# A two-block transformer on one core: the pooling sums and the mean subtraction of the mixers move from GpSimd to VectorE

## The chip, the cores and the metric

The kernel runs on one core of a Trainium2 chip, in one launch. The metric is the device time of the whole program in microseconds (us). Engines are written as the profile writes them: PE (TensorE matmul), PEld (TensorE weight load), DVE (VectorE), ACT (ScalarE), POOL (GpSimd), SP (SyncE, which here only issues DMAs).

## The reference, cut to what matters

A first transformer block (two layers) and a second one (two layers) are worked one after the other in float32 on 256 tokens of 1024 channels. Only the first block is touched. Each of its layers is a feed-forward network, a mixer, and a second feed-forward network, each followed by a layer norm of a weighted sum of input and output; 16 learned tokens are put ahead of the 256, so that the rows are 272 long. The mixer has three branches over one projection of its input:

```python
z = h @ w_in
xp, ca, cg, q, k, v, g = jnp.split(z, splits, axis=-1)
y_pool = pool_mixer(xp, pool_w, pool_scale)      # trailing means over 2, 4, 8, 16 tokens, minus the token
y_conv = conv_module(ca, cg, ...)                # 31-tap causal depthwise convolution, norm, projection
y_ret = retention(q, k, v, g, ret_gn_g)          # four heads with a decay, then a norm per head
return jnp.concatenate([y_pool, y_conv, y_ret], axis=-1) @ w_out
```

The pooling branch takes, for each of four groups of 64 channels, the mean over the last 2, 4, 8 or 16 tokens, subtracts the token itself and multiplies the result with a small matrix.

## The kernel before, in words

Every engine has its own instruction stream, written out by hand and run in order; the streams are tied by semaphores (`then_inc` when an instruction is done, `wait_ge` ahead of one that needs it). There is no planner: the place of a line in an engine's stream is its order.

Activations lie channel-major: 128 partitions by 8 tiles of channels (`CT`) by 272 tokens (`L1`). Weights stream as "units" of 1 MB (128 x 2048 float32). For each unit SP issues a DMA into one of four slots of `RAW`, ACT rounds it to `WHI` (function `high`, L1430), and DVE subtracts to get the low part `WLO` (function `rest`, L1975). Each product is three matmuls: high by high, high by low, low by high (function `three`). A slot is loaded again when PE has finished the unit in it.

A mixer has 15 units, `u0` to `u0 + 14`. PE's stream in it (function `mixer` under `block.tensor`) is: units 0 and 1 (the convolution's input and gate), units 2 to 5 (queries and keys), units 6 and 7 (values, token-major) with `scores(0)` and `scores(1)` of the retention heads behind them, unit 8 (the pooling branch's input), `values(0)`, `scores(2)`, `values(1)`, unit 9 (half of the output gate), the pooling product "pooled" (`PW` by `PM`), `scores(3)`, `values(2)`, the mean of the convolution's output (`ONES` by `ACC`, semaphore `cv_mean`), the first tile of unit 10, the variance (`ONES` by `CSG`, semaphore `cv_var`), `values(3)`, the second tile of unit 10, the variance of the heads (`ONES` by `OSQ`), the convolution's projection, and units 11 to 14, the output projection, with the sums for the norm after them.

`scores(h)` writes a head's scores into PSUM banks 4 to 6, so that `scores(h)` waits until DVE has taken the scores of head h - 1 out of them (DVE function `decay(h - 1)`, L2192 and L2193, semaphore `ret_decayed`). The mean of the convolution waits for all 62 taps (semaphore `conv_tap`) and for the low parts of the pooling output (`YPL`, L2252, semaphore `y_low`).

DVE's stream in a mixer (function `mixer` under `block.vector`) interleaves four things: `rest` of each unit, the 62 taps of the convolution (`taps(a, b)`, L2171, two instructions of 128 x 272 for each tap), the rotation of queries and keys (`rotate(n)`, L2182 to L2186), and `decay(h)`. In the part that matters its order is `taps(7, 14)`, `decay(0)`, `centre_values(0)`, `taps(14, 21)`, `rest(u0 + 10)`, `centre_values(1)`, `decay(1)`, `rest(u0 + 11)`, `taps(21, 28)`, `decay(2)`, `taps(28, 31)`, `rest(u0 + 12)`, the two `YPL`, `decay(3)`, and then the norms of the convolution and of the heads (`CSTD`, L2262; `GSTD`, L2269; `GS`, L2278; `XLO`, L2272 and L2281).

POOL works in a mixer: the loads of tables, `add_halves` (L521, L524: sum over the channels' tiles in `SUM1`, for a mean that PE takes and ACT copies to `MH`), `shift_x` (L532: four instructions, `PL = XL - MH`, after all four rotations, since the rotation's scratch tiles lie in `PL`), the pooling windows (L586 to L593), and, after the output projection, `add_tiles` (L543). The windows need `XP`, which ACT copies out of PSUM when unit 8 is done (L1562). They are four running sums, each of the one before it (windows of 2, 4, 8, 16 tokens, `PT_`), four products with the inverse counts on 64 partitions each (`WN`), and one subtraction (`PM`): nine instructions, counted by the semaphore `pool_step`, on which PE's pooling product waits. `PL` is needed by `take_tiles` (L2055), which adds the output projection to it, and waits on `x_shifted`.

A `Steps` object counts instructions on one semaphore; `link` issues an instruction and waits for it, `did` only counts it:

```python
def link(self, ins):
    self.did(ins)
    self.wait()
```

Of the kernel before, what the change touches and what calls it, by code (L numbers as in the profile page):

```python
# [11 lines left out]
ALU = mybir.AluOpType  # L12
# [12 lines left out]
L1 = META + SEQ  # L25
# [22 lines left out]
POOL_STEPS = 9  # L48
# [23 lines left out]
def build(nc, A, out):  # L72
    with ExitStack() as ctx:
        def sem(name):
            return ctx.enter_context(nc.semaphore(name))
# [42 lines left out]
        XL = X[:, :, X0:L2]  # L118
# [7 lines left out]
        MH = norm.put("MH", [L1])  # L126
# [32 lines left out]
        IC = mixb.put("IC", [2, L1])  # L159
        PW = mixb.put("PW", [2, P])  # L160
        PWC = mixb.put("PWC", [4, P])
        XP = mixb.put("XP", [2, 16 + L1])
        YPH = place("B", "YPH", mixb.at, [2, L1], F32R)
        YPL = place("B", "YPL", mixb.at + 2 * L1, [2, L1], F32R)
        PT_ = [mixb.put(f"PT{n}", [2, 16 + L1]) for n in range(4)]
        WN = mixb.put("WN", [2, L1])
        PM = mixb.put("PM", [2, L1])
# [128 lines left out]
        def tokens(q):  # L296


            return slice(META if q >= 4 else 0, L1)
# [7 lines left out]
        def conv_at(i, f):  # L307
# [12 lines left out]
        half_added, half_mean, half_copied, x_shifted = (sem("half_added"), sem("half_mean"), sem("half_copied"),  # L320
                                                         sem("x_shifted"))
# [5 lines left out]
        tab1_loaded, pads_set = sem("tab1_loaded"), sem("pads_set")  # L327
        conv_gate, conv_in, conv_tap, rot_step, rotated = (sem("conv_gate"), sem("conv_in"), sem("conv_tap"),
                                                           sem("rot_step"), sem("rotated"))
# [3 lines left out]
        xp_copied, pool_step, pooled = sem("xp_copied"), sem("pool_step"), sem("pooled")  # L333
# [41 lines left out]
        for n in range(UNITS1):  # L375
            l, m = n // UNITS_LAYER, n % UNITS_LAYER
# [73 lines left out]
        def bc(t, n):  # L450
            return t.rearrange("p (o n) -> p o n", o=1).to_broadcast([P, n, t.shape[-1]])
# [42 lines left out]
        def _(pool):  # L494
# [3 lines left out]
            def ada_load(h):  # L498
                if h >= ADA_RING:
                    pool.wait_ge(ada_step, 8 * (h - ADA_RING + 1))  # L500
                pool.dma_start(AW[:, h % ADA_RING, :, :], A["ada"][h, :, :].rearrange("p (k c) -> p k c", k=4))\
                    .then_inc(ada_loaded[h % ADA_RING], 16)
# [24 lines left out]
            def shift_x(q):  # L527

                pool.wait_ge(half_copied, q + 1)
                tk = tokens(q)  # L530
                for c in range(4):
                    pool.tensor_tensor(PL[:, 2 * c:2 * c + 2, tk], XL[:, 2 * c:2 * c + 2, tk], bc(MH[:, tk], 2),  # L532
                                       ALU.subtract).then_inc(x_shifted, 1)
# [29 lines left out]
            def mixer(l):  # L563
                q, base = 3 * l + 1, POOL_STEPS * l
                pool.wait_ge(ada_done, 6 * (2 * l + 1))
                for dst, src in ((RC[:, :], A["rope_c"]), (RS[:, :, :], A["rope_s"]), (DT[:, :, :, :], A["decay"]),
                                 (IC[:, :, :], A["inv_count"]), (PW[:, :, :], A["pool_w"][l, :, :, :]),
                                 (PWC[:, :, :], A["conv_pw"][l, :, :, :])):
                    pool.dma_start(dst, src).then_inc(tab1_loaded, 16)
                pool.wait_ge(tile_out, 8 * q)  # L570
                pool.memset(CP[:, :, 0:TAPS - 1], 0.0).then_inc(pads_set, 1)
                pool.memset(XP[:, :, 0:16], 0.0).then_inc(pads_set, 1)
                for t in PT_:
                    pool.memset(t[:, :, 0:16], 0.0).then_inc(pads_set, 1)
                add_halves(q)
                pool.wait_ge(rotated, 4 * l + 4)
                shift_x(q)
                pool.wait_ge(xp_copied, l + 1)
                pool.wait_ge(pads_set, 6 * (l + 1))
                pool.wait_ge(tab1_loaded, 16 * 6 * (l + 1))  # L580
                st = Steps(pool, pool_step, base, POOL_STEPS)
                src, n = XP, 16 + L1
                for j in range(4):
                    w = 1 << j
                    lo = 2 * w - 1
                    st.link(pool.tensor_tensor(PT_[j][:, :, lo:n], src[:, :, lo:n], src[:, :, lo - w:n - w], ALU.add))  # L586
                    src = PT_[j]
                for j in range(4):
                    q64 = slice(64 * (j % 2), 64 * (j % 2) + 64)
                    st.did(pool.tensor_tensor(WN[q64, j // 2, :], PT_[j][q64, j // 2, 16:n], IC[q64, j // 2, :],  # L590
                                              ALU.mult))
                st.wait()
                st.did(pool.tensor_tensor(PM[:, :, :], WN[:, :, :], XP[:, :, 16:n], ALU.subtract))  # L593
                st.end()
                add_tiles(q)
                for h in range(ADA_RING):
                    if h == 2:
                        pool.wait_ge(tile_out, 8 * q + 8)
                    ada_load(12 * (2 * l + 1) + h)
# [35 lines left out]
            for odd in range(2):  # L635
                pool.wait_ge(pool2_step, QUERY_SET - 2 + odd)
                q = slice(64 * odd, 64 * odd + 64)
# [18 lines left out]
            for n in range(2):  # L656
                for odd in range(2):
                    pool.wait_ge(pool2_step, HEADS_ZERO + 2 * n + odd)
                    q = slice(64 - 64 * odd, P - 64 * odd)
# [1306 lines left out]
        def _(v):  # L1966
            v.memset(MODF[:, :, :], 0.0).then_inc(start_set, 1)

            def rest(n):

                if n >= UNITS:
                    return
                s = slot_of[n]
                v.wait_ge(w1_high, highs[n])
                v.tensor_tensor(WLO1[:, s, :], RAW[:, s, :], WHI1[:, s, :].bitcast(F32), ALU.subtract)\  # L1975
                    .then_inc(w1_split, 1)
# [39 lines left out]
            def pair(c, tk):  # L2016
                return PL[:, 2 * c:2 * c + 2, tk]
# [135 lines left out]
            def mixer(l):  # L2153
                q = 3 * l + 1
# [7 lines left out]
                def taps(a, b):  # L2162
                    for t in range(a, b):
                        for j in range(2):
                            w = VEC[:, V_DW + 2 * t + j:V_DW + 2 * t + j + 1]
                            if t == 0:
                                ins = v.tensor_scalar(ACC[:, j, :], CP[:, j, 0:L1], w,
                                                      VEC[:, V_DB + j:V_DB + j + 1], ALU.mult, ALU.add)
                            else:
                                v.wait_ge(conv_tap, l * 62 + (2 * t + j - 1))  # L2170
                                ins = v.scalar_tensor_tensor(ACC[:, j, :], CP[:, j, t:t + L1], w, ACC[:, j, :],  # L2171
                                                             ALU.mult, ALU.add)
                            ins.then_inc(conv_tap, 1)
# [22 lines left out]
                def centre_values(z):  # L2196
# [10 lines left out]
                        last = v.tensor_tensor(o, o, m, ALU.add)  # L2207
                    last.then_inc(v_centred, 1)

                def head_gain(h):  # L2210
                    v.wait_ge(ret_squared, 4 * l + h + 1)
                    v.wait_ge(gs_done, 2 * l + h // 2 + 1)
                    v.scalar_tensor_tensor(GS[:, h, :], OT[:, h, :], VEC[:, V_GN + h:V_GN + h + 1], GS[:, h, :],
                                           ALU.mult, ALU.mult).then_inc(gn_z, 1)
# [28 lines left out]
                centre_values(1)  # L2243
                decay(1)
                rest(u0 + 11)
                taps(21, 28)
                decay(2)
                taps(28, 31)
# [9 lines left out]
                head_gain(0)  # L2258
                head_gain(1)
                rest(u0 + 13)  # L2260
                v.wait_ge(cv_std, l + 1)
                v.reciprocal(CSTD[:, :], CSTD[:, :]).then_inc(cv_rstd, 1)  # L2262
                v.wait_ge(cv_rstd, l + 1)
                v.wait_ge(cv_squared, l + 1)
                v.tensor_tensor(ACC[:, :, :], ACC[:, :, :], bc(CSTD[:, :], 2), ALU.mult).then_inc(cv_normed, 1)
                head_gain(2)
                head_gain(3)
                v.wait_ge(gn_std, l + 1)
                v.reciprocal(GSTD[:, :], GSTD[:, :]).then_inc(gn_rstd, 1)  # L2269
                for t in range(2):  # L2270
                    v.wait_ge(y_high, 8 * l + 3 + t)
                    v.tensor_tensor(XLO1[:, 2 + t, :], PS[:, t, 0:L1], XHI1[:, 2 + t, :].bitcast(F32), ALU.subtract)\  # L2272
                        .then_inc(y_low, 1)
                for h in range(RH + 1):
                    if h < RH:
                        v.wait_ge(gn_spread, 4 * l + h + 1)
                        v.wait_ge(gn_z, 4 * l + h + 1)
                        v.tensor_tensor(GS[:, h, :], GS[:, h, :], PS[:, 4 + h, 0:L1], ALU.mult).then_inc(gn_y, 1)  # L2278
                    if h >= 1:
                        v.wait_ge(y_high, 8 * l + 4 + h)  # L2280
                        v.tensor_tensor(XLO1[:, 3 + h, :], GS[:, h - 1, :], XHI1[:, 3 + h, :].bitcast(F32),  # L2281
                                        ALU.subtract).then_inc(y_low, 1)
# [565 lines left out]
```

## Time and profile before

| what | value |
|---|---|
| median of 3 runs | 2326.58 us (2322.51 to 2329.9) |
| the profiled execution's own time | 2322.65 us |
| span of its profile | 2320.9 us |
| granted TensorE clock, mean over the span | 0.969 |
| PE busy | 2216.4 us, 96% of the span |
| PEld busy | 2030.0 us, 87% |
| DVE busy | 1611.2 us, 69% |
| ACT busy | 1046.7 us, 45% |
| POOL busy | 209.8 us, 9% |
| bytes moved | 333.86 MB, mean 144 GB/s |

The span is the time from the first to the last instruction that the profile holds; the execution's own time is 1.75 us longer. Busy shares are means over all stages, so the stretches of the two mixers are read by themselves: the first lies at about 240 to 385 us, the second at about 820 to 960 us of the span. A granted clock of 1.00 is TensorE's 2.4 GHz, one of 0.50 is 1.2 GHz; a number between them is a stretch that had both.

### The profile page before, as it was taken

The page shows a single profiled execution, that of the slowest core. Times are in us where ns is not written, and L with a number is a line of the kernel's source. Part 1 is how long each engine was busy: PE and PEld are TensorE (multiplying, and loading weights), DVE is VectorE, ACT ScalarE, POOL GpSimd, SP SyncE. Part 2 cuts the span into 40 slices and gives each one's busy share as a digit, 9 for nine tenths or more (in the row PEclk, how much of TensorE's full clock was granted, in tenths as well). Part 3 has the DMA queues.
Part 4 walks back from the last instruction along what each step waited for, and adds up shares of the span by engine and source line. Part 5 has one row for each costly group of instructions (what it writes and reads, how often), then busy time and mean ns, then how long its engine had stood idle before and what let it go on. Part 6 is the DMA issues. An engine that isn't in the chain of part 4 may idle for free. (4 is left out here: it accounts for less than half of the span.)

```text
span 2320.9 us, 35981 instructions
## 1 busy us (share of the span) xinstructions
PE 2216.4 (96%) x15136; PEld 2030.0 (87%) x15136; DVE 1611.2 (69%) x2407; ACT 1046.7 (45%) x1512; POOL 209.8 (9%) x219
## 2 busy tenths in 40 slices
PE   6999998999999999899999998999999997997997
PEld 6999978999999997899999776698888886687997
DVE  5878886877887789697853467666455437757774
ACT  5433535433544344444444335534444323755662
POOL 2100232100210023210100001000000000100000
PEclk9999989999999999999998999999999998998998
DMA  5665524667466552476522112022322222113552
GB/s 212 241 218 204 193 73 152 241 224 255 182 220 218 199 193 85 186 256 236 201 91 79 55 55 79 19 73 91 105 95 91 104 78 74 54 42 115 186 177 100
DMA packets 47488, 333.86 MB, mean 144 GB/s; under 512 B 5532, under 2 KB 6652, under 8 KB 7776
## 3 DMA queue, kind: packets, MB, share of 16 engines
q1 hardware_dynamic: 37808, 268.45, 32.3%
q0 software_dynamic: 9520, 63.11, 7.3%
q8 instruction: 120, 1.97, 0.3%
q14 instruction: 40, 0.33, 0.0%
HBM read 330.50 MB, written 1.05 MB: 143 GB/s over the span
## 5 line engine op out<-in xcount | busy, mean ns | idle before, releaser
L1975 DVE TENSOR_TENSOR WLO<-RAW,WHI 128x2048 fp32r<-128x2048 f32 x252 | 587.9, 2335 | 269.4 <-ACT WHI L1430 266.6
L448 PE MATMUL PS<-XB,WHI 128*128 128x256 f32 (+1 forms) x3072 | 701.0, 323 | 15.5 <-DVE XB L2320 10.7
L1430 ACT CAST WHI<-RAW 128x2048 fp32r<-128x2048 f32 x252 | 479.8, 1907 | 317.8 <-DMA RAW<-in_dn_c 79.8
L448 PEld LDWEIGHTS PS<-XB,WHI 128*128 128x128 f32 x3072 | 517.4, 192 | 62.8 <-issue 18.1
L448 PE MATMUL PS<-XHI,WHI 128*128 128x272 f32 (+1 forms) x1792 | 523.3, 295 | 18.3 <-ACT XHI L1438 14.9
L448 PE MATMUL PS<-XHI,WLO 128*128 128x272 f32 (+1 forms) x1792 | 518.1, 292 | 0.0
L448 PE MATMUL PS<-XLO,WHI 128*128 128x272 f32 (+1 forms) x1792 | 495.2, 290 | 0.0
L448 PE MATMUL PS<-XB,WLO 128*128 128x256 f32 (+1 forms) x1536 | 494.0, 322 | 0.0
L448 PEld LDWEIGHTS PS<-XHI,WHI 128*128 128x128 f32 x1792 | 346.3, 193 | 23.8 <-issue 18.8
L448 PEld LDWEIGHTS PS<-XHI,WLO 128*128 128x128 f32 x1792 | 345.8, 193 | 0.0
L448 PEld LDWEIGHTS PS<-XLO,WHI 128*128 128x128 f32 x1792 | 334.1, 192 | 0.4
L448 PEld LDWEIGHTS PS<-XB,WLO 128*128 128x128 f32 x1536 | 294.9, 192 | 21.1
L2006 DVE SCALAR_TENSOR_TENSOR AP<-AW,SC,AP 128x512 f32<-128x512 f32 x336 | 241.5, 770 | 0.0
L448 PE MATMUL PS<-GHI,WLO 128*128 128x272 f32 (+1 forms) x704 | 201.3, 286 | 0.0
L448 PE MATMUL PS<-GHI,WHI 128*128 128x272 f32 (+1 forms) x704 | 201.2, 286 | 0.0
L448 PE MATMUL PS<-GLO,WHI 128*128 128x272 f32 (+1 forms) x704 | 201.0, 285 | 0.0
L2364 DVE SCALAR_TENSOR_TENSOR AC<-CB,FCW,AC 128x512 f32<-128x512 f32 (+1 forms) x176 | 97.1, 614 | 134.0 <-ACT AC L1658 103.8
L1487 ACT ACTIVATE SG<-PS 128x272 f32<-128x272 f32 (+1 forms) x88 | 34.2, 394 | 224.4 <-PE PS L448 224.4
L448 PEld LDWEIGHTS PS<-GHI,WHI 128*128 128x128 f32 x704 | 132.5, 188 | 0.0
L448 PEld LDWEIGHTS PS<-GHI,WLO 128*128 128x128 f32 x704 | 132.4, 188 | 0.0
L448 PEld LDWEIGHTS PS<-GLO,WHI 128*128 128x128 f32 x704 | 132.4, 188 | 0.0
L1656 ACT COPY CB<-PS 128x512 f32<-128x512 f32 x52 | 27.9, 589 | 114.0 <-PE PS L448 114.0
(362 smaller groups left out, 2735.1 us busy)
## 6 DMA issues: line engine op xcount, KB each, us to landing
AW<-in_ada POOLq DMA_DIRECT2D x48, 1024.0 KB, 6.7
RAW<-in_up_a SPq DMA_DIRECT2D x44, 1024.0 KB, 4.9
RAW<-in_up_b SPq DMA_DIRECT2D x44, 1024.0 KB, 4.9
RAW<-in_up_c SPq DMA_DIRECT2D x44, 1024.0 KB, 4.9
RAW<-in_mix SPq DMA_DIRECT2D x30, 1024.0 KB, 4.9
RAW<-in_dn_a SPq DMA_DIRECT2D x22, 1024.0 KB, 4.9
RAW<-in_dn_b SPq DMA_DIRECT2D x22, 1024.0 KB, 4.9
RAW<-in_dn_c SPq DMA_DIRECT2D x22, 1024.0 KB, 4.8
```

Of the source, the lines that this page charges most:

```text
L448: return pe.matmul(o, w, x, start=first, stop=last)
L1430: act.copy(WHI1[:, s, :], RAW[:, s, :]).then_inc(w1_high, 1)
L1487: act.activation(SG[:, f % 2, tk], PS[:, 2 * (f % 3), tk], ACT.Silu).then_inc(silu1_done, 1)
L1656: act.copy(cb[:, a, :, 1:257], two(PS[:, banks + a, :]))
L1975: v.tensor_tensor(WLO1[:, s, :], RAW[:, s, :], WHI1[:, s, :].bitcast(F32), ALU.subtract)\
L2006: v.scalar_tensor_tensor(a, w, c, a, ALU.mult, ALU.add).then_inc(ada_step, 1)
L2364: return v.scalar_tensor_tensor(o, i, vec(a, t), o, ALU.mult, ALU.add)
```

## The change

POOL's stream in `mixer` loses `shift_x` and the nine instructions of the pooling windows, with their waits. DVE's stream in `mixer` gets both. The windows stand, in the same form, as `pool_windows()` between `rest(u0 + 11)` and `taps(21, 28)`. The subtraction of the mean is split in its four instructions, `shift(0)` to `shift(3)`: one behind `rest(u0 + 13)`, one behind the normed convolution (L2265), and two behind the low parts of the convolution's output (L2272). The feed-forward networks keep `shift_x` on POOL, and `add_halves`, `add_tiles` and all table loads stay where they are. Shapes, operands and the number of instructions are the same.

```diff
--- before.py
+++ after.py
@@ -573,25 +573,6 @@
                 for t in PT_:
                     pool.memset(t[:, :, 0:16], 0.0).then_inc(pads_set, 1)
                 add_halves(q)
-                pool.wait_ge(rotated, 4 * l + 4)
-                shift_x(q)
-                pool.wait_ge(xp_copied, l + 1)
-                pool.wait_ge(pads_set, 6 * (l + 1))
-                pool.wait_ge(tab1_loaded, 16 * 6 * (l + 1))
-                st = Steps(pool, pool_step, base, POOL_STEPS)
-                src, n = XP, 16 + L1
-                for j in range(4):
-                    w = 1 << j
-                    lo = 2 * w - 1
-                    st.link(pool.tensor_tensor(PT_[j][:, :, lo:n], src[:, :, lo:n], src[:, :, lo - w:n - w], ALU.add))
-                    src = PT_[j]
-                for j in range(4):
-                    q64 = slice(64 * (j % 2), 64 * (j % 2) + 64)
-                    st.did(pool.tensor_tensor(WN[q64, j // 2, :], PT_[j][q64, j // 2, 16:n], IC[q64, j // 2, :],
-                                              ALU.mult))
-                st.wait()
-                st.did(pool.tensor_tensor(PM[:, :, :], WN[:, :, :], XP[:, :, 16:n], ALU.subtract))
-                st.end()
                 add_tiles(q)
                 for h in range(ADA_RING):
                     if h == 2:
@@ -2207,6 +2188,34 @@
                         last = v.tensor_tensor(o, o, m, ALU.add)
                     last.then_inc(v_centred, 1)
 
+                def shift(c):
+
+                    tk = tokens(q)
+                    v.wait_ge(half_copied, q + 1)
+                    v.wait_ge(rotated, 4 * l + 4)
+                    v.tensor_tensor(pair(c, tk), XL[:, 2 * c:2 * c + 2, tk], bc(MH[:, tk], 2), ALU.subtract)\
+                        .then_inc(x_shifted, 1)
+
+                def pool_windows():
+
+                    v.wait_ge(xp_copied, l + 1)
+                    v.wait_ge(pads_set, 6 * (l + 1))
+                    v.wait_ge(tab1_loaded, 16 * 6 * (l + 1))
+                    st = Steps(v, pool_step, POOL_STEPS * l, POOL_STEPS)
+                    src, n = XP, 16 + L1
+                    for j in range(4):
+                        w = 1 << j
+                        lo = 2 * w - 1
+                        st.link(v.tensor_tensor(PT_[j][:, :, lo:n], src[:, :, lo:n], src[:, :, lo - w:n - w], ALU.add))
+                        src = PT_[j]
+                    for j in range(4):
+                        q64 = slice(64 * (j % 2), 64 * (j % 2) + 64)
+                        st.did(v.tensor_tensor(WN[q64, j // 2, :], PT_[j][q64, j // 2, 16:n], IC[q64, j // 2, :],
+                                               ALU.mult))
+                    st.wait()
+                    st.did(v.tensor_tensor(PM[:, :, :], WN[:, :, :], XP[:, :, 16:n], ALU.subtract))
+                    st.end()
+
                 def head_gain(h):
                     v.wait_ge(ret_squared, 4 * l + h + 1)
                     v.wait_ge(gs_done, 2 * l + h // 2 + 1)
@@ -2243,6 +2252,7 @@
                 centre_values(1)
                 decay(1)
                 rest(u0 + 11)
+                pool_windows()
                 taps(21, 28)
                 decay(2)
                 taps(28, 31)
@@ -2258,11 +2268,13 @@
                 head_gain(0)
                 head_gain(1)
                 rest(u0 + 13)
+                shift(0)
                 v.wait_ge(cv_std, l + 1)
                 v.reciprocal(CSTD[:, :], CSTD[:, :]).then_inc(cv_rstd, 1)
                 v.wait_ge(cv_rstd, l + 1)
                 v.wait_ge(cv_squared, l + 1)
                 v.tensor_tensor(ACC[:, :, :], ACC[:, :, :], bc(CSTD[:, :], 2), ALU.mult).then_inc(cv_normed, 1)
+                shift(1)
                 head_gain(2)
                 head_gain(3)
                 v.wait_ge(gn_std, l + 1)
@@ -2271,6 +2283,8 @@
                     v.wait_ge(y_high, 8 * l + 3 + t)
                     v.tensor_tensor(XLO1[:, 2 + t, :], PS[:, t, 0:L1], XHI1[:, 2 + t, :].bitcast(F32), ALU.subtract)\
                         .then_inc(y_low, 1)
+                shift(2)
+                shift(3)
                 for h in range(RH + 1):
                     if h < RH:
                         v.wait_ge(gn_spread, 4 * l + h + 1)
```

## Rows read from the trace of the kernel before

**Rows 1.** The page: busy time, share of the span and instructions of the engines.
```profile
PE 2216.4 (96%) x15136; PEld 2030.0 (87%) x15136; DVE 1611.2 (69%) x2407; ACT 1046.7 (45%) x1512; POOL 209.8 (9%) x219
```

**Rows 2.** Waits of PE, 245 to 400 us: waited for, us in total, times, longest.
```profile
PE PS L448 <- DVE ST L2193: 3.1, 2, 2.6
```

**Rows 3.** PE in order, first mixer: start, us, instruction, count, [idle before <-releaser].
```profile
314.21 3.11 PE L448 MATMUL PS<-QK 64*128 64x272 f32 x12 [0.48 <-DVE ST L2193]
...
325.46 1.18 PE L448 MATMUL PS<-PM,PW 128*128 128x272 f32 x4
329.22 5.91 PE L448 MATMUL PS<-QK 64*128 64x272 f32 x12 [2.57 <-DVE ST L2193]
...
344.47 1.08 PE L448 MATMUL PS<-CSG,ONES 128*128 128x272 f32 x4
```

**Rows 4.** The same of the second mixer.
```profile
893.73 4.02 PE L448 MATMUL PS<-QK 64*128 64x272 f32 x12 [0.32 <-DVE ST L2193]
...
909.36 1.08 PE L448 MATMUL PS<-PM,PW 128*128 128x272 f32 x4
910.37 3.11 PE L448 MATMUL PS<-QK 64*128 64x272 f32 x12
...
915.18 1.18 PE L448 MATMUL PS<-ACC,ONES 128*128 128x272 f32 x4
919.22 1.08 PE L448 MATMUL PS<-CSG,ONES 128*128 128x272 f32 x4
```

**Rows 5.** Stretches: busy us of PE, PEld, DVE, ACT, POOL; PEclk; DMA share; GB/s.
```profile
312.00:326.00 14.00, 13.39 (x76) 10.13 (x75) 13.97 (x16) 5.79 (x8) 11.90 (x9) 1.00 0.21 76
326.00:346.00 20.00, 17.43 (x56) 11.70 (x55) 13.46 (x23) 5.81 (x8) 0.00 (x0) 0.66 0.15 53
...
896.00:906.00 10.00, 10.00 (x32) 6.98 (x31) 10.00 (x11) 3.87 (x4) 8.30 (x8) 0.50 0.02 7
```

**Rows 6.** DVE in order, first mixer.
```profile
292.51 9.17 DVE L2171 SCALAR_TENSOR_TENSOR ACC<-CP,VEC,ACC 128x272 f32<-128x272 f32 x14
...
303.85 5.85 DVE L2171 SCALAR_TENSOR_TENSOR ACC<-CP,VEC,ACC 128x272 f32<-128x272 f32 x14
...
316.28 11.90 DVE L2171 SCALAR_TENSOR_TENSOR ACC<-CP,VEC,ACC 128x272 f32<-128x272 f32 x14
328.11 0.71 DVE L2192 TENSOR_TENSOR ST<-PS,DT 128x544 f32<-128x544 f32 x1
...
331.56 2.27 DVE L1975 TENSOR_TENSOR WLO<-RAW,WHI 128x2048 fp32r<-128x2048 f32 x1
333.76 0.89 DVE L2252 SCALAR_TENSOR_TENSOR YPL<-PS,VEC,YPH 128x272 fp32r<-128x272 f32 x2
```

**Rows 7.** POOL in order, first mixer.
```profile
287.09 9.75 POOL L532 TENSOR_TENSOR PL<-X,MH 128x544 f32<-128x544 f32 x4 [29.25 <-DVE QK L2186]
312.89 1.29 POOL L586 TENSOR_TENSOR PT<-XP 128x574 f32<-128x574 f32 x1 [16.05 <-ACT XP L1562]
...
323.97 1.44 POOL L593 TENSOR_TENSOR PM<-WN,XP 128x544 f32<-128x544 f32 x1
```

**Rows 8.** ACT in order: the copy of XP, first and second mixer.
```profile
312.20 0.61 ACT L1562 COPY XP<-PS 128x544 f32<-128x544 f32 x1 [2.57 <-PE PS L448]
...
891.88 0.61 ACT L1562 COPY XP<-PS 128x544 f32<-128x544 f32 x1 [2.57 <-PE PS L448]
```

**Rows 9.** DVE in order, around the rotation (first mixer) and the convolution's norm (second).
```profile
268.81 0.43 DVE L2184 TENSOR_TENSOR T<-PS,RS 128x272 f32<-128x272 f32 x1
269.28 0.72 DVE L2186 TENSOR_TENSOR QK<-T,T 128x544 f32<-128x544 f32 x1
...
920.86 1.85 DVE L2262 RECIPROCAL CSTD<-CSTD 128x272 f32<-128x272 f32 x1 [0.70 <-ACT CSTD L1577]
...
925.85 0.92 DVE L2213 SCALAR_TENSOR_TENSOR GS<-OT,VEC,GS 128x272 f32<-128x272 f32 x2 [2.38 <-ACT GS L1584]
...
935.34 0.79 DVE L2278 TENSOR_TENSOR GS<-GS,PS 128x272 f32<-128x272 f32 x2 [5.27 <-PE PS L448]
```

## The prediction

> **What bounds the kernel now.** I read the page's busy line first: PE is busy for 96% of the span, POOL for 9% [rows 1]. A POOL that is nearly idle is not the bound by its own time, so the change can only pay where POOL's work delays PE, by itself or through DVE. Next I read PE's waits in the stretch of the first mixer. One of them goes back to this change's neighbourhood: 3.1 us for DVE's `ST`, which is `decay(h)`, 2.6 us of it in one wait [rows 2]. PE in order says where: after the pooling product at 325.46 PE has nothing to do until `scores(3)` at 329.22 [rows 3]. In the second mixer the same `scores(3)` follows the pooling product without a gap, at 910.37 [rows 4]. The reader is to see that PE does not wait for POOL's result as such (the pooling product stands where unit 9 ends), but for DVE behind it.
>
> The view by stretches shows a second cost: the granted clock is 1.00 from 312 to 326 us and 0.66 on the mean from 326 to 346 [rows 5]. The twelve matmuls of `scores(3)` take 5.91 us behind the 2.57 us gap, against 3.11 for the same twelve in the second mixer [rows 3, 4]. The second mixer has a fall too, elsewhere: 0.50 from 896 to 906, behind `scores(2)`, which waited for 0.32 us, and while unit 9 ran [rows 4, 5].
>
> Then DVE in order. Fourteen instructions of the taps cost 5.85 us where POOL is idle (303.85), but 9.17 us beside POOL's subtraction of the mean and 11.90 us beside its windows [rows 6, 7]. Same line, same shape, same count: the difference, 3.3 + 6.05 = 9.4 us for each mixer, is what POOL costs DVE. The other mixer has the same pattern.
>
> **The change, part by part.** I count in microseconds from the start of ACT's copy of `XP`, which is 312.20 in the first mixer and 891.88 in the second [rows 8], since both engines are tied to unit 8 there.
>
> Removed: `shift_x` and the windows leave POOL: 9.75 us, and 12.5 us from 312.89 to the end of `PM` at 325.41 [rows 7]. By themselves they are hidden behind PE's units; what they give back is the slowing of DVE.
>
> Added on DVE, windows: a 128x544 with both inputs in SBUF takes 0.72 us, and one that needs the result of the instruction just before starts 0.04 us after its end (268.81 + 0.43 = 269.24, started at 269.28) [rows 9]. Four linked sums: 4 x 0.76 = 3.0. Four products on 64 partitions, at most the 0.43 us of a 128x272 each: 1.7 with no link between. Then `PM`: 0.76. Together 5.5 us. The trace shows no window on DVE, so bounds: below, nine instructions at 0.43, 3.9 us; above, POOL's own 12.5 us for the same nine [rows 7]. I take 5.5, since the 0.72 row has the same kind and size of operands.
>
> Added on DVE, shifts: 4 x 0.72 = 2.9 us. `shift(0)` stands ahead of the wait for the convolution's deviation, where DVE is idle for 0.70 us at full clock; `shift(1)` has a pause of 2.38, `shift(2)` and `shift(3)` one of 5.27 behind them [rows 9]. I cost all four at nothing. If the cover of the first is gone the norm of the convolution is up to 0.7 us later in each mixer. `PL` is needed only by `take_tiles`, after the output projection, so `x_shifted` holds nobody up.
>
> Added wait: DVE now waits for `XP` with `taps(21, 28)` and `decay(2)` queued behind. The 3.3 us of `taps(7, 14)` bring DVE there at 316.28 - 3.3 = 313.0 at the latest, a little earlier if the weight split beside the shift is slowed too; the copy ends at 312.81 [rows 6, 8]. The two meet, so the wait costs about nothing, and I let the windows start at +0.66.
>
> DVE after: windows +0.66 to +6.15; fourteen taps at 5.85 to +12.0; `decay(2)` and six taps 3.45 (328.11 to 331.56), of which `decay(2)` about 1.0, so it is done at +13.0 and the taps at +15.45; `rest(u0 + 12)` 2.2 (331.56 to 333.76) to +17.65; both `YPL` 0.9 to +18.55 [rows 6].
>
> PE after, at clock 1.00: `scores(2)` started 2.01 after `XP` and waited for 0.48 of it; `decay(1)` is now early, so +1.53. From there to the pooling product 11.25 (314.21 to 325.46): +12.78 [rows 3]. `scores(3)` 1.01 later, +13.79; the mean of the convolution 4.81 behind that, +18.60; its variance 4.04 later, +22.64 [rows 4]. DVE's `decay(2)` is ready 0.8 us and `YPL` 0.05 us before PE comes for them. Nothing stalls PE there, with little to spare; an error of 1 us in my windows costs about 1 us at the mean and still none at `scores(3)`.
>
> The sum: the variance stood 32.27 after `XP` in the first mixer (344.47 - 312.20), now 22.64: 9.6 us. In the second 27.34 (919.22 - 891.88), now 22.64: 4.7 us [rows 3, 4, 8]. With PE at full clock all through, 14.3 us. Behind the variance the chain is that of before.
>
> That needs both falls of the clock to go. The one of the first mixer comes behind the 2.57 us gap, which goes. The one of the second comes in a stretch that keeps its short matmuls and loses a gap of only 0.3 us; the first mixer ran that same stretch at 1.00, so one in two shows it. A fall there costs 15.63 - 11.25 = 4.4 us (893.73 to 909.36 against 314.21 to 325.46) [rows 3, 4]. I take one such fall in the two mixers: 14.3 - 4.4 = 9.9, rounded to 10 us.
>
> The gain is carried to the end because PE, with 96%, is the bound behind the mixers and the weights are prefetched as PE frees slots. The profiled execution took 2322.65 us, 1.75 over its span of 2320.9, and is 3.9 below the median of the runs, 2326.58. By its own time I get 2312.6; against the median, 2316.6, which I predict.
>
> The Trainium skill (SBUF — State Buffer, Who interferes with whom) says that a DVE instruction with two SBUF inputs and a GpSimd instruction that reads SBUF contend for one port as an exclusive lock, held for a whole instruction. The rows agree that such taps are slowed, by 0.43 us each on the mean in the windows' stretch. By the rule in its strictest form DVE could have been shut out for all of POOL's 12.5 us there, and DVE would get back up to that; the rows show 6.05 us. Since PE is next in line either way, the sum would be the same; what the rule adds is that the slowing has no other cause that stays.
>
> **The rivals.**
>
> *Both mixers at full clock.* No fall is left: 14.3 us, 2312.3 against the median. For it: the pauses that PE had are nearly all gone. Against it: the fall in the second mixer came with hardly a pause ahead.
>
> *The clock falls in both mixers.* The stretch from `scores(2)` to unit 9 runs at 0.50 in each: 14.3 - 8.8 = 5.5 us, 2321.1. For it: PE's arrival is moved by some 10 us and the second mixer shows a fall with little reason. Against it: the first had none.
>
> *Slower: the taps stay slow.* If what slows the taps were not POOL but the place in the mixer (transfers, ACT beside them), the fourteen taps behind the windows still take 11.9. Then `decay(2)` is done at 13.0 + 6.05 = +19.05, where PE waited until +17.02 before (329.22 - 312.20) [rows 3, 6]. The first mixer ends 2.0 us later. In the second PE would wait from about +13.8 or +18.2 and get the gap that the first has, with its fall: the difference of the two mixers before, 32.27 - 27.34 = 4.9, and the same 2.0. Together 8.9 us slower, 2335.5. It decides where the windows and the taps together exceed 17.0 - 0.66 - 1.0 = 15.3 us; I have 11.35. Windows on DVE at 9.5 us instead of 5.5 would do it too. Against it: the taps at 303.85, between the two stretches, are at full speed while transfers and ACT run.
>
> *No change.* DVE does what it should, but the gain is lost before the end of the span, at a wait on transfers or on a clock that falls later. Against it: PE's share. Price: within 3 us of 2326.6.
>
> **How the numbers follow.** Chances: one fall left 0.45, none 0.22, both 0.18, no change 0.08, slower 0.07. From 2326.58, 0.3% is 7 us; less than that a measurement can't tell from no change. Faster takes the first two cases and a tenth of the third: 0.69. Within takes the rest of the third, no change, and a little of slower: 0.25. Slower: 0.06. The range reaches from 2308, the case with none and 4 us for the spread of the runs, to 2323, the case with both and 2 us.
>
> **What would show it.** In the changed trace: `taps(7, 14)`, and the fourteen behind the windows, at 5.85 us; nine instructions of the windows on DVE in 5.5 us, beginning about 0.7 us after the start of the copy of `XP`; no wait of PE for `ST` at `scores(3)`; the variance 22 to 23 us after `XP` in a mixer without a fall, 27 with one; shifts in idle time, with the reciprocal of `CSTD` not later behind the variance than before. The prediction is wrong if the windows take over 9 us, if the taps keep 11.9, if PE waits at `scores(3)`, or if clock falls in other stretches take the gain back.

## The result and the profile after

The change makes the kernel faster: 2311.12 us against 2324.1 (medians of 6 runs each), ratio 0.9934, interval 0.9918 to 0.9949; the ratios here are estimated from the single runs, and the quotient of the two medians is 0.9944. Run again beside the experiments the change came to 0.9928 (0.9912 to 0.9945). Three executions far outside all others (3404.82 and 12225.14 us of the kernel before, 3639.64 us of one variant) are left out of the ratios. The profiled execution took 2311.72 us, with a span of 2309.9 and a mean clock of 0.973 (before 2322.65, 2320.9 and 0.969). Forecast were 10 us less and 2316.6 us, range 2308 to 2323.

The page's busy line answers to [rows 1]: POOL lost 43 us of busy time, DVE took on 26 more instructions and is busy for 4 us less than before.

```profile
PE 2206.0 (96%) x15136; PEld 2023.8 (88%) x15136; DVE 1606.9 (70%) x2433; ACT 1046.0 (45%) x1512; POOL 166.7 (7%) x193
```

DVE in order in the first mixer, to be held against [rows 6]. Lines are those of the changed kernel: L2152 taps, L2209 to L2216 windows, L2196 `shift`. A tap is two instructions, so `taps(21, 28)` shows as x14; below, "fourteen taps" and "six taps" count instructions.

```profile
291.38 5.86 DVE L2152 SCALAR_TENSOR_TENSOR ACC<-CP,VEC,ACC 128x272 f32<-128x272 f32 x14
...
312.29 0.76 DVE L2209 TENSOR_TENSOR PT<-XP 128x574 f32<-128x574 f32 x1 [0.40 <-ACT XP L1543]
313.08 2.29 DVE L2209 TENSOR_TENSOR PT<-PT 128x570 f32<-128x570 f32 x3
315.41 1.84 DVE L2213 TENSOR_TENSOR WN<-PT,IC 64x272 f32<-64x272 f32 x4
317.29 0.73 DVE L2216 TENSOR_TENSOR PM<-WN,XP 128x544 f32<-128x544 f32 x1
317.93 5.86 DVE L2152 SCALAR_TENSOR_TENSOR ACC<-CP,VEC,ACC 128x272 f32<-128x272 f32 x14
323.70 0.72 DVE L2173 TENSOR_TENSOR ST<-PS,DT 128x544 f32<-128x544 f32 x1
...
329.36 0.89 DVE L2262 SCALAR_TENSOR_TENSOR YPL<-PS,VEC,YPH 128x272 fp32r<-128x272 f32 x2
...
335.25 0.72 DVE L2196 TENSOR_TENSOR PL<-X,MH 128x544 f32<-128x544 f32 x1
336.06 1.85 DVE L2273 RECIPROCAL CSTD<-CSTD 128x272 f32<-128x272 f32 x1
```

The windows take 5.6 us (312.29 to 317.93), both groups of fourteen taps 5.86, and the first subtraction ends just before the reciprocal that it might have delayed. The reciprocal starts 336.06 - 334.42 = 1.64 us after the variance, as it did before (920.86 - 919.22).

PE in order, first mixer, with ACT's copy of `XP` first; this answers to [rows 3] and [rows 8].

```profile
311.64 0.61 ACT L1543 COPY XP<-PS 128x544 f32<-128x544 f32 x1 [2.38 <-PE PS L448]
```
```profile
313.11 3.11 PE L448 MATMUL PS<-QK 64*128 64x272 f32 x12
...
324.06 1.08 PE L448 MATMUL PS<-PM,PW 128*128 128x272 f32 x4
325.07 3.11 PE L448 MATMUL PS<-QK 64*128 64x272 f32 x12
...
330.40 1.16 PE L448 MATMUL PS<-ACC,ONES 128*128 128x272 f32 x4 [0.45 <-DVE YPL L2262]
334.42 1.08 PE L448 MATMUL PS<-CSG,ONES 128*128 128x272 f32 x4
```

Neither `scores(2)` nor `scores(3)` waits. The variance of the convolution stands 334.42 - 311.64 = 22.78 us after the copy, where it stood at 32.27; in the second mixer 904.56 - 881.80 = 22.76, before 27.34. Both mixers together: 9.5 + 4.6 = 14.1 us.

One small wait for POOL's result goes too. In the first mixer before, the last matmul of unit 9 started at 325.05, `PM` was done at 325.41 and the pooling product started at 325.46 [rows 3, 7]; in the changed kernel the product follows that matmul within 0.13 us (323.94, 324.06). The two lines, before and after:

```profile
325.05 0.29 PE L448 MATMUL PS<-XHI,WLO 128*128 128x272 f32 x1
```
```profile
323.94 0.29 PE L448 MATMUL PS<-XHI,WLO 128*128 128x272 f32 x1
```

The spans differ by 11.0 us only. Most of the rest is lost far behind, in the attention of the second block: the same ACT instruction starts 14.4 us earlier at its beginning (1365.83 before, 1351.44 after) and 11.6 us earlier at its end (1486.27, 1474.67). Stretches of the kernel before, then of the changed one, laid so that both begin with the same work (columns as in [rows 5]):

```profile
1410.00:1460.00 50.00, 40.23 (x219) 26.37 (x218) 35.07 (x110) 30.52 (x88) 2.66 (x5) 0.99 0.20 70
1460.00:1500.00 40.00, 38.24 (x220) 28.29 (x219) 25.45 (x69) 22.78 (x54) 0.15 (x2) 0.97 0.08 27
```
```profile
1396.00:1446.00 50.00, 40.65 (x214) 27.61 (x214) 34.52 (x107) 29.96 (x88) 2.67 (x5) 0.95 0.20 70
1446.00:1486.00 40.00, 38.92 (x208) 27.90 (x208) 24.87 (x67) 21.04 (x51) 0.00 (x0) 0.93 0.08 27
```

The granted clock is 0.95 and 0.93 there, 0.99 and 0.97 before. No instruction of that stretch was changed, and the changed kernel's second profiled execution did not have that fall: 0.99 and 0.97 in 1398 to 1448 and 1448 to 1488 us, with a span of 2305.7 us, 15.2 us below the span before. The ratio of the runs, 0.66% or 15 us (12 to 19), leaves room for the whole 14. The kernel before was traced once only, so how often its mixers show the two falls is not known.

### The profile page after: what moved, and what is told of

It is laid out like the page before. It is cut to its first block and busy times, and to the rows that moved or that the text cites. A ratio compares the mean times of both kernels' runs of the same rounds, so it can differ in the third digit from the quotient of the medians.

```text
span 2309.9 us, 35987 instructions
## 1 busy us (share of the span) xinstructions
PE 2206.0 (96%) x15136; PEld 2023.8 (88%) x15136; DVE 1606.9 (70%) x2433; ACT 1046.0 (45%) x1512; POOL 166.7 (7%) x193
## 5 line engine op out<-in xcount | busy, mean ns | idle before, releaser
L448 PE MATMUL PS<-XB,WHI 128*128 128x256 f32 (+1 forms) x3072 | 701.0, 323 | 17.6 <-DVE XB L2334 12.1
```

What stands on the lines that cost most here:

```text
L448: return pe.matmul(o, w, x, start=first, stop=last)
```

## The experiments

My first theory was the prediction's: DVE is late at `decay(2)` and `YPL`, whatever makes it late. The rival: it matters which of POOL's two pieces goes.

**One half of the change at a time.** First the subtraction alone on DVE.

```diff
 def mixer(l):                      # POOL
-    pool.wait_ge(rotated, 4 * l + 4)
-    shift_x(q)
 ...                                # DVE: shift(0) to shift(3) as in the change; windows stay on POOL
```

> Only the four subtractions of the mean go to VectorE (at the changed kernel's places); the pooling windows stay on GpSimd. Theory (VectorE's lateness at decay(2) and YPL is what costs, whichever of GpSimd's two pieces causes it): taps(7, 14) fall from 9.2 to 5.9 us, VectorE reaches taps(21, 28) some 3.5 us earlier, these still take 11.9 us beside the windows, decay(2) is done about +13.8 us after the start of the copy of XP, PE's gap of 2.57 us at scores(3) shrinks to 0.5 or less, and the variance of the convolution stands at about +23.5 us (before +32.3 and +27.3; after the change +22.8). That is 8.8 + 3.8 = 12.6 us, a ratio of 0.9946. Rival (the windows, the larger piece beside the taps, are what costs): the ratio is 1.000 and the gap stays.

Measured: ratio 1.0044 (1.0025 to 1.0063), slower than before. `taps(7, 14)` took 5.86 us, as the theory said, and the gap at `scores(3)` was gone, but `decay(2)` was done at +6.9 us and not at +13.8, since `taps(21, 28)` were not slowed either. PE had a new wait. POOL and then DVE in order, first mixer:

```profile
315.22 6.22 POOL L584 TENSOR_TENSOR PT<-XP 128x574 f32<-128x574 f32 x1 [56.49 <-ACT XP L1560]
321.52 4.10 POOL L584 TENSOR_TENSOR PT<-PT 128x570 f32<-128x570 f32 x3
325.69 5.46 POOL L588 TENSOR_TENSOR WN<-PT,IC 64x272 f32<-64x272 f32 x4
331.23 1.33 POOL L591 TENSOR_TENSOR PM<-WN,XP 128x544 f32<-128x544 f32 x1
```
```profile
314.58 5.85 DVE L2169 SCALAR_TENSOR_TENSOR ACC<-CP,VEC,ACC 128x272 f32<-128x272 f32 x14
320.36 0.70 DVE L2190 TENSOR_TENSOR ST<-PS,DT 128x544 f32<-128x544 f32 x1
320.99 0.42 DVE L2191 TENSOR_TENSOR ST<-PS,DT 16x272 f32<-16x272 f32 x1
321.34 6.44 DVE L2169 SCALAR_TENSOR_TENSOR ACC<-CP,VEC,ACC 128x272 f32<-128x272 f32 x6
```

DVE reached the taps just before POOL began. This time the fourteen taps ran at full speed and POOL's first sum, 1.29 us before [rows 7], took 6.22: it ended at 321.44, 1.0 us after the last of the fourteen. Then six taps took 6.44. The two engines shut each other out, and either can be the one that pays. The kernel before shows it too: POOL's second sum took 3.1 us there, beside a `rest` on DVE that kept its 2.27 us. Which engine pays is not explained by the recorded starts: the fourteen taps began 0.64 us ahead of POOL's first sum and it paid, the six began 0.18 us ahead of its second and they paid. `PM` was done 18.0 us after the start of the copy instead of 13.2, and PE waited for it:

```profile
PE PS L448 <- POOL PM L591: 5.5, 1, 5.5
```

The variance stood at +35.81 and +35.88 us, 12.1 us later in the two mixers together; the median lost 12.5.

Then the windows alone.

```diff
-    rest(u0 + 11)                  # DVE; the nine instructions leave POOL, shift_x stays there
-    taps(21, 28)
+    rest(u0 + 11)
+    pool_windows()
+    taps(21, 28)
```

> Only the nine instructions of the pooling windows go to VectorE; the subtraction of the mean stays on GpSimd. Theory (lateness): VectorE arrives at the windows at +4.1 us as before, since taps(7, 14) still take 9.2 us; 5.6 us of windows and 5.9 of taps put decay(2) at +16.6, nearly where it was (+17.0), so the gap of about 2.5 us at scores(3) stays and with it a clock fall; the variance stands at about +31.5 in the first mixer. Ratio 1.000, between 0.998 and 1.002. Rival (the windows are what costs): ratio near that of the whole change, 0.9934, and no gap.

Measured: ratio 0.9998 (0.9986 to 1.001), as the theory had it, though its mechanism was not the one seen. There was no gap at `scores(3)`, because PE was late too: it waited for `scores(2)` and ran it and unit 9 at the lower clock.

```profile
316.01 4.12 PE L448 MATMUL PS<-QK 64*128 64x272 f32 x12 [0.47 <-DVE ST L2176]
...
331.62 1.08 PE L448 MATMUL PS<-PM,PW 128*128 128x272 f32 x4
```

The variance stood at +27.47 and +27.25 us, what the second mixer had before; +31.5 was expected in the first. So the trace has 4.9 us of gain in the mixers, and the times at most 3.3; where the difference goes is open. In the times neither half brings anything; the whole brings 0.66%.

**No move at all, only another order on DVE.**

```diff
-    taps(21, 28)
+    taps(21, 24)
     decay(2)
+    taps(24, 28)
     taps(28, 31)
-    rest(u0 + 12)
     ...                            # the two YPL and decay(3)
+    rest(u0 + 12)
```

> The kernel before with nothing moved between engines; only VectorE's order is changed: taps(21, 24) ahead of decay(2) and the other taps behind it, and rest(u0 + 12) behind decay(3) instead of ahead of YPL. Theory (lateness): the taps beside GpSimd stay slow (0.85 us each), but decay(2) is done at about +10.3 and YPL at about +18.6 us, so PE has no gap there; the variance stands at about +23.2. 9 + 4 = 13 us, ratio 0.9944, without giving GpSimd any relief. Rival (the contention of GpSimd with VectorE has to go): ratio 1.000.

Measured: ratio 1.0033 (1.0014 to 1.0052). The theory falls here: the variance stood at +29.05 and +28.80 us where +23.2 was expected. `decay(2)` was done at +12.1, ahead of PE, but POOL was starved again: `PM`, one instruction of 1.44 us before, waited out the fourteen taps behind `decay(2)`.

```profile
325.98 7.25 POOL L593 TENSOR_TENSOR PM<-WN,XP 128x544 f32<-128x544 f32 x1
```
```profile
326.18 5.84 DVE L2171 SCALAR_TENSOR_TENSOR ACC<-CP,VEC,ACC 128x272 f32<-128x272 f32 x14
```

The profiled execution, 2321.47 us, is among the fastest of its twelve, whose median is 2333.26, so the usual run loses more than this trace shows: eight of the twelve took 2330 us or more, and what they lose is open. In each order tried with the windows on POOL, DVE's taps or POOL's `PM` is late, and PE needs both.

**The contention by itself.** The changed kernel, with work for POOL beside DVE's windows and taps that hardly anything waits for: additions that read SBUF, or memsets that only write it.

```diff
+    for j in range(9):             # POOL, from the copy of XP on
+        ...                        # each behind the one before, counted by a semaphore
+        pool.tensor_tensor(PL[:, 0:2, :], XL[:, 0:2, :], XL[:, 2:4, :], ALU.add)
+        # the other kernel: pool.memset(PL[:, 0:6, :], 0.0)
```

> The changed kernel, and beside it GpSimd adds two tiles of X into scratch nine times (128x544, two SBUF inputs) from the copy of XP on; nothing but the first subtraction of the mean waits for it. Theory (contention of a GpSimd that reads SBUF with VectorE instructions with two SBUF inputs): VectorE's windows take 9 to 11 us instead of 5.5 or the taps behind them 8 instead of 5.9, 5 to 6 us lost in all, decay(2) is done at +18, PE gets its gap of 4 to 5 us back; variance at +30 or later; ratio 0.999 to 1.003. Rival (the taps were slow for where they stand, not for GpSimd): windows and taps keep 5.5 and 5.9 us, ratio 0.9934.

> The same with nine memsets of 128x1632 by GpSimd (some 1.4 us each, it writes and reads nothing) in place of the nine additions. If the contention is for reading SBUF alone, windows and taps keep 5.5 and 5.9 us and the ratio is 0.9934. If any work of GpSimd slows VectorE, windows and taps are slowed as beside the additions and the ratio is 0.999 or more.

Measured: additions 1.0054 (1.0033 to 1.0075), memsets 0.9937 (0.992 to 0.9954). DVE beside the additions, then beside the memsets:

```profile
315.18 0.76 DVE L2217 TENSOR_TENSOR PT<-XP 128x574 f32<-128x574 f32 x1 [0.56 <-ACT XP L1550]
315.97 5.35 DVE L2217 TENSOR_TENSOR PT<-PT 128x570 f32<-128x570 f32 x3
321.36 6.03 DVE L2221 TENSOR_TENSOR WN<-PT,IC 64x272 f32<-64x272 f32 x4
327.43 1.74 DVE L2224 TENSOR_TENSOR PM<-WN,XP 128x544 f32<-128x544 f32 x1
329.09 6.93 DVE L2159 SCALAR_TENSOR_TENSOR ACC<-CP,VEC,ACC 128x272 f32<-128x272 f32 x14
```
```profile
313.89 2.29 DVE L2217 TENSOR_TENSOR PT<-PT 128x570 f32<-128x570 f32 x3
316.22 1.84 DVE L2221 TENSOR_TENSOR WN<-PT,IC 64x272 f32<-64x272 f32 x4
318.09 0.73 DVE L2224 TENSOR_TENSOR PM<-WN,XP 128x544 f32<-128x544 f32 x1
318.74 5.87 DVE L2159 SCALAR_TENSOR_TENSOR ACC<-CP,VEC,ACC 128x272 f32<-128x272 f32 x14
```

Beside POOL's reads the windows take 13.9 us (315.18 to 329.09) instead of 5.6; beside 13.6 us of memsets windows and taps keep their 5.6 and 5.87. PE had a gap of 6.64 us at `scores(3)` in the first, and one of 2.10 for `PM` ahead of it. Windows and ratio came out above the 9 to 11 us and the 1.003 that were expected at most. Of the two kinds of work only the one that reads SBUF slows DVE; they also differ in kind, an addition and a memset, and no other pair was tried. The Trainium skill says so too (SBUF — State Buffer, Who interferes with whom): with two SBUF inputs DVE contends with a GpSimd that reads SBUF, not with one that only writes it. The 13.9 us beside the additions and the 5.6 us beside the memsets agree. It also says that the order of issue decides who is blocked. The 6.22 us sum, recorded behind the first of the taps, agrees; the 7.25 us `PM` does not by its recorded start, 325.98, which lies 0.2 us ahead of the taps that it waited out (326.18). The runs leave it open how the two take turns.

**The price of the windows.** The same nine instructions worked twice on DVE.

```diff
+    for again in range(2):
         ...                        # four sums, four products, PM
+        st.wait()
```

> The changed kernel with the nine instructions of the windows worked twice on VectorE, same result. It asks for the break-even of the windows' price. Theory (lateness): 5.6 us more put decay(2) at +18.3 us and PE, which is ready at +13.4, waits for about 5 us with a fall of the clock behind it; YPL is done at +24, the mean of the convolution follows at +24.5 at the earliest, the variance at +32 to +34. That is 9 to 11 us more than the changed kernel in each mixer: ratio 1.001 to 1.004 (slower than before, since both mixers have the gap). Rival (VectorE has slack enough to take such work): ratio 0.994 to 0.997.

Measured: ratio 1.0024 (1.0011 to 1.0037). Only the time of this variant is read. It bears out that some 5.6 us more than the change adds turn the gain into a loss.

**The wait at `scores(2)`.** In the traces so far the clock fell at `scores(2)` only in mixers in which PE had waited for `decay(1)`. So I put that wait back into the changed kernel, with the same work on DVE, and took it out of the kernel before.

```diff
     centre_values(1)
-    decay(1)
     rest(u0 + 11)
+    taps(21, 22)                   # the longer one: taps(21, 23)
+    decay(1)
     pool_windows()
-    taps(21, 28)
+    taps(22, 28)
```

> The changed kernel with decay(1) behind rest(u0 + 11) and taps(21, 22) instead of ahead of them: the same work on VectorE, but PE waits some 0.3 to 0.4 us for decay(1) at scores(2), as it did before the change (0.48 and 0.32 us). New theory (that short wait, which GpSimd's subtraction of the mean caused by slowing taps(7, 14), is what brought the clock fall of scores(2) and unit 9, seen in five of the six mixers that have the wait and in none of the twelve that have not): the clock falls there in both mixers, the variance stands at about +27 us instead of +22.8, and some 8 us are lost: ratio 0.996 to 0.998 to the kernel before. Rival (falls are chance, as the prediction had it): variance at +23.1 in most mixers, ratio 0.9935.

> The same with taps(21, 23) ahead of decay(1): a wait of some 1.2 us at scores(2). New theory: the same fall in both mixers, variance at +27.5 to +28, ratio 0.997 to 0.999. Rival (the wait costs its own length alone): variance at +24, ratio 0.9945.

Measured: short 0.9936 (0.9922 to 0.9949), long 0.9954 (0.994 to 0.9968). The short one missed its aim: `scores(2)` began at +1.56 and +1.59 us where it begins at +1.47 without a wait, so it waited for 0.1 us, and the clock stayed. The long one waited for 0.94 us in both mixers. PE in order in the first, then in the second:

```profile
315.30 5.04 PE L448 MATMUL PS<-QK 64*128 64x272 f32 x12 [0.94 <-DVE ST L2174]
...
331.01 1.08 PE L448 MATMUL PS<-PM,PW 128*128 128x272 f32 x4
```
```profile
889.14 3.12 PE L448 MATMUL PS<-QK 64*128 64x272 f32 x12 [0.94 <-DVE ST L2174]
...
900.10 1.08 PE L448 MATMUL PS<-PM,PW 128*128 128x272 f32 x4
```

The same wait brought the fall in one mixer, variance at +28.0, and not in the other, +23.3. The ratio, 4 us over the change, lies between the two expectations; the traced execution is the fastest of the five, and whether the others had more falls is not shown.

```diff
+    centre_values(1)               # the kernel before, nothing moved between engines
+    decay(1)
     rest(u0 + 10)
-    centre_values(1)
-    decay(1)
```

> The kernel before with centre_values(1) and decay(1) ahead of rest(u0 + 10): the wait at scores(2) goes, GpSimd keeps its work. New theory: no fall at scores(2) in either mixer, but decay(2) is as late as before, so both mixers now have the gap of 2.5 to 3 us at scores(3) with the fall behind it, that only the first had; the variance stands at about +32 in both (before +32.3 and +27.3). Ratio 1.001 to 1.003. Rival (removing the wait at scores(2) alone is a gain): ratio 0.998 or less.

Measured: ratio 1.0019 (1.0009 to 1.003), as expected; the variance stood at +32.70 and +32.72. Both mixers ran `scores(2)` at full clock and then had pauses of 2.4 and 2.1 us for POOL's `PM` and 1.74 for `decay(2)`, with the fall behind them. Ahead of POOL's first sum DVE now had two `rest` in a row, and that sum took 4.94 us in the first mixer, so moving `decay(1)` also made `PM` later. PE in order, second mixer:

```profile
906.43 1.19 PE L448 MATMUL PS<-PM,PW 128*128 128x272 f32 x4 [2.09 <-POOL PM L593]
909.35 5.91 PE L448 MATMUL PS<-QK 64*128 64x272 f32 x12 [1.74 <-DVE ST L2193]
```

**YPL earlier, and a version meant to beat both.** `rest(u0 + 12)` behind `decay(3)`; then also the two `XLO` ahead of the reciprocal of `GSTD`.

```diff
     ...                            # the two YPL
     decay(3)
+    rest(u0 + 12)                  # was ahead of YPL
     ...
+    ...                            # only in the second: XLO of the convolution's two tiles, moved up
     v.reciprocal(GSTD[:, :], GSTD[:, :]).then_inc(gn_rstd, 1)
```

> The changed kernel with rest(u0 + 12) behind decay(3) instead of ahead of the two YPL. Theory (lateness): YPL is done 2.2 us earlier, PE's wait of 0.45 us for it ahead of the mean of the convolution goes in both mixers, the variance stands at about +22.3 us (+22.8 in the changed kernel); ratio 0.9930, which the clock can't be told from 0.9934, so the trace decides. Rival (those 0.45 us are worth nothing, since something else is late next): the variance stays at +22.8.

> A version meant to beat both: the changed kernel with rest(u0 + 12) behind decay(3), and the two low parts of the convolution's output (XLO) ahead of the reciprocal of GSTD. PE's wait of 0.92 us for XLO in the output projection goes in both mixers (the reciprocal is not needed for another 5 us), and its wait of 0.45 us for YPL. Ratio 0.992 if the two waits are worth their length, 2.8 us in all; 0.9935 if the clock or the next wait takes them back.

Measured: the first 0.9937 (0.992 to 0.9953), variance at +22.28 in both mixers as expected; the half microsecond can't be told in the time. The second 0.9915 (0.9899 to 0.993), 2305.72 us: PE's wait of 0.92 us in the output projection was gone, and this is the fastest kernel of the study by its ratio, though the interval overlaps that of the change. The change itself was not run beside it; the short variant above, whose trace differs from it by under 0.1 us at the variance, was at 0.9936 (2309.68 us) there, so the two edits are worth some 4 us where 2.8 were expected; the intervals overlap, and whether there is more to it stays open.

## Why the prediction was right, and where it was off

- *What slows DVE.* Right: both groups of taps came back to 5.86 us, and the memsets and additions show the cause.
- *The windows' price.* 5.5 us forecast, 5.6 measured. They began at +0.65, forecast +0.66.
- *The shifts at nothing.* Right: 335.25 to 335.97 lies in the time in which DVE would have waited for ACT, and the instructions behind the other three kept their places after the variance (`GS` at +6.63, before +6.62, and at +16.37, before +16.36).
- *DVE's and PE's times.* `YPL` was forecast for +18.55 and was done at 330.25 - 311.64 = +18.61. `scores(3)` was forecast for +13.79 and came at +13.43, since PE goes from `scores(2)` to the pooling product in 10.95 us, not 11.25. So PE was ready earlier than `YPL` and waited for 0.45 us. The variance: +22.64 forecast, +22.78 and +22.76 measured.
- *PE and POOL's result.* The prediction held that PE does not wait for POOL's result as such. In the first mixer before it did, for 0.3 us, which is why 11.25 us stood there for the 10.95 of full clock; and `shift_only`, `order_only` and `early_decay1` show PE waiting 1.2 to 5.7 us for `PM` as soon as POOL is shut out or PE is early.
- *One fall of the clock left.* This is the term that was mis-sized: 4.4 us were taken off, none was due. All four mixers of the change that were traced ran the stretch at full clock. I had read the fall in the second mixer as chance. In the traces it came in six of the eight mixers in which PE waited for 0.23 us or more at `scores(2)`, and in none of the eighteen in which it did not or for 0.1 us. That wait was POOL's doing as well: `shift_x` slowed `taps(7, 14)`, which made `decay(1)` late. Whether such a wait brings the fall is not certain (the long variant shows both), but without it there was none. The first rival, both mixers at full clock with 14.3 us, is what happened. It had been given 0.22. That the time still lies well inside the range is in part luck: some 3 us of the mixers' gain were lost in other stretches, for which the forecast had no term.
- *How the time is carried.* 14.1 us in the mixers; 11.0 in the first pair of spans, 15.2 with the second trace of the change; 13.0 in the medians, 16.1 in those of the second comparison. The forecast of 2316.6 started from 2326.58, a median of three; with six it is 2324.1, which is 2.5 of the 5.5 us by which the forecast time was high.
- *What the prediction did not see.* It took POOL's 12.5 us for the windows as fixed. They are not: POOL is shut out as well, 17.3 us from the first sum to the end of `PM` in `shift_only` (315.22 to 332.56). So the halves don't add up (+0.44%, -0.02%, together -0.66%), and the idea that relieving DVE by a mere change of order would do was wrong.

## What to carry to other kernels

Where two engines slow each other, time each of them with the other idle before an operation is moved, and don't take either one's duration as fixed: half a move can starve the engine that keeps its half. Here an operation of 12.5 us on the slow engine cost 5.6 on the fast one, and its presence beside the fast one had cost 6: moving it added nothing to the fast engine's time. Read a short wait of PE together with the granted clock behind it: here waits of 0.2 to 2.6 us were mostly followed by a stretch at half clock that cost 4 to 6 us more than the same matmuls at full clock.

## What the runs showed of the hardware

- GpSimd additions and VectorE instructions with two SBUF inputs exclude each other, in both directions: a 1.3 us addition took 6.22 us and a 1.4 us subtraction 7.25 us, each until about its own length after the end of fourteen tap instructions; the six that take 2.54 us elsewhere took 6.44 in turn. Which of the two engines is held up did not follow from the recorded starts.
- GpSimd memsets of 1.5 us beside the same VectorE instructions cost them nothing.
- A wait of 0.94 us on TensorE was followed by a fall to 1.2 GHz in one mixer (mean granted clock 0.70 over 314 to 331 us) and by 2.4 GHz in the next (1.00 over 888 to 905), with the same instructions around it.
